# Identity matmuls of TensorE ahead of nine of its waits, in a kernel of three layers

## The chip, the core and the metric

The kernel runs on one core of a Trainium2 chip. The metric is the device time of one execution in microseconds; lower is better. The engines are named as in the profile: PE is TensorE's matmuls and PEld its weight loads, DVE is VectorE, ACT is ScalarE, POOL is GpSimd, SP issues DMAs.

## The reference

256 tokens of width 2048 pass through an attention layer, a retention layer and a second block (attention of two kinds, then a feed-forward with a convolution), everything in float32. Cut to what matters:

```python
def first_block(x, ...):
    x = layer_norm(ALPHA * x + attention_mixer(x, ...), gain[0], bias[0])   # 16 heads of 128, 4 kv heads
    x = layer_norm(ALPHA * x + retention_mixer(x, ...), gain[1], bias[1])   # 8 heads, 256 and 512 wide
    return x

def second_block(x, c, ...):
    mod = silu(c) @ w_mod + b_mod                      # six rows of 2048
    h = rms_norm(x, norm_attn) * (1 + sc1) + sh1
    x = x + g1 * (concat(swa_attention(...), dsa_attention(...)) @ w_out)
    h = rms_norm(x, norm_ffn) * (1 + sc2) + sh2
    u, g = split(h @ w_up)                             # 2 x 5632 columns
    x = x + g2 * ((silu(causal_conv3(u) + conv_b) * g) @ w_down)
    return rms_norm(x, norm_final)
```

Every projection `h @ w` is computed by the kernel as a sum of three products of rounded parts, `x_hi w_hi + x_hi w_lo + x_lo w_hi`.

## The kernel before, in words

Weights are cut into blocks of 2048x512 (some narrower), and a block into four chunks of 512 rows. For every chunk SP issues two DMAs into `raw`, ScalarE rounds it to `w_hi` (`round_hi`, line 389), VectorE subtracts to get `w_lo` (`split_lo`, line 394, written over `raw`), and TensorE multiplies (`product`, lines 400 to 402; `project` for the x-side projections, `output` for those behind a head). A chunk of `project` is 4 slices x 2 token tiles x 3 products = 24 matmuls of 128x512. `raw`, `w_hi` and `w_lo` hold four chunks; SP waits for TensorE's semaphore `products` before it loads one anew. Each engine has its own queue, written out by hand, and works it in order; semaphores tie them together.

TensorE's queue is that of `pe_first_block` and `pe_second_block`. Attention has a first step written out (`pe_attention(pe, 0)`) and a loop over the other three key-value heads; then come the last head's transposes (`pe_a_turn`) and output (`pe_a_output`). `turn_groups` brings the activations into the layout for products: eight groups of four 128x128 results, in six banks in turn (`turn[0]`, `turn[1]`, `sc[0]`, `sc[1]`, `pair[1][0]`, `pair[1][1]`), as plain transposes (line 466) or as f32 matmuls with the diagonal matrix `diag` (line 464), which scales as it transposes. VectorE turns each group to `x_mid` (line 496), ScalarE rounds it to `x_hi` (line 477), VectorE makes `x_lo` (line 483), and the first chunk of the next product waits for two groups' `x_lo`. Retention has the same form as attention, with eight steps. In its first step VectorE also scales the residual rows (`vec_residual`) before it splits the next block's fourth chunk. The second block follows: `diag` of the first RMS norm, projections, index and attention heads, output, `diag` of the second, and the feed-forward in 11 steps (`pe_feed_forward`), whose last output is `pe_f_output(pe, FG)`; it waits for `f_hl`, which comes from `f_h` by way of `f_hh`, and `f_h` from the convolution (`f_conv`).

The matrix `ident` is 128x128 f32 in SBUF. The banks are PSUM banks of 128x512 f32; eight exist: two `pair`s of two, two `turn`, two `sc`.

The calls of TensorE's queue that the change stands among, with the lines of before:

```python
            if first:                                   # in pe_attention
                for c in range(CH):
                    between(c)
            else:
                pe_a_output(pe, i, between)
...
                            mm = pe.matmul(to, src, diag[:, t, :], start=True, stop=True)   # L464
                        else:
                            mm = pe.transpose(to, src, ident[:, :])                         # L466
```

Of the kernel before, what the change touches and what calls it, by code (L numbers as in the profile page):

```python
# [25 lines left out]
P = 128  # L26
# [13 lines left out]
FG = FF // CB  # L40
# [75 lines left out]
def build(nc, x, attn_w_in, attn_q_gain, attn_k_gain, attn_w_out, ret_w_in, ret_decay_exp,  # L116
# [5 lines left out]
    with ctx:  # L122
# [24 lines left out]
        ident = take("ident", [P])  # L147
# [126 lines left out]
        def bank(name):  # L274
            return ctx.enter_context(nc.psum_tensor(name, [P, CB], F32))

        pair = [[bank("pair0_t0"), bank("pair0_t1")], [bank("pair1_t0"), bank("pair1_t1")]]
        turn = [bank("turn0"), bank("turn1")]
        sc = [bank("sc0"), bank("sc1")]
# [3 lines left out]
        def sem(name):  # L283
            if name not in S:
                S[name] = ctx.enter_context(nc.semaphore(name))
            return S[name]
# [216 lines left out]
        def pe_transposes(pe, to, src, tiles):  # L503
# [4 lines left out]
                    mm = pe.transpose(to[:, i * P:(i + 1) * P], src[:, t, m * P:(m + 1) * P], ident[:, :])  # L508
            return mm

        def pe_mod(pe, step):

            pe.wait_ge(sem("mod_used"), 8 * step + 8)
            for q in range(8):
                mm = pe.matmul(sc[0][:, q:q + 1], m_acc[:, q * P:(q + 1) * P],  # L515
                               ones[:, 0:1], start=True, stop=True)
            mm.then_inc(sem("mod_cols"), 1)
# [5 lines left out]
        def pe_a_output(pe, i, after=None):  # L523

            last = isinstance(i, int) and i == A_KV

            def before(c):
                if c == 0:
                    pe.wait_ge(sem("a_ol"), 2 * i)
                    pe.wait_ge(sem("a_sg"), i if last else i + 1)  # L530
                elif c == 1:
                    if not last:
                        pe.wait_ge(sem("a_krot"), i + 1)
                else:
                    pe.wait_ge(sem("a_sum_z"), 2 + 4 * (i - 1) + c - 1)
            output(pe, a_block(i, 0) if last else a_block(i, 3), a_oh, a_ol, [0, 1, 0, 1], before, after)

        def pe_a_turn(pe, i):

            pe.wait_ge(sem("a_og"), i)  # L540
            for b in range(2):
                pe_transposes(pe, turn[b], a_og, [2 * b, 2 * b + 1]).then_inc(sem("a_turned"), 1)

        def pe_attention(pe, i):
# [84 lines left out]
            def between(c):  # L629

                if c == 1:
                    turn_probs(0)
                    turn_probs(1)
                elif c == 2:
                    pe.wait_ge(sem("a_prob"), 4 * i + 4)
                    values(0)
                    turn_probs(2)
                    values(1)
                    turn_probs(3)
                elif c == 3:  # L640
                    values(2)
                    values(3)
            project(pe, a_block(i, 2), pair[0], before=q_read, after=along_gate)
            if first:
                for c in range(CH):
                    between(c)
            else:
                pe_a_output(pe, i, between)

# [19 lines left out]
        def pe_r_output(pe, i, after=None):  # L669
            last = isinstance(i, int) and i == R_HEADS  # L670

            def before(c):
                if c == 0:
                    pe.wait_ge(sem("r_ol"), 2 * i)
                    pe.wait_ge(sem("r_sg"), i if last else i + 1)
                elif c == 1:
                    if not last:
                        pe.wait_ge(sem("r_v"), i + 1)
                else:
                    pe.wait_ge(sem("r_sum_z"), 2 + 4 * (i - 1) + c - 1)  # L680
            output(pe, r_block(i, 0) if last else r_block(i, 3), r_oh, r_ol, [0, 1, 0, 1], before, after)

        def pe_r_turn(pe, i):
            pe.wait_ge(sem("r_og"), i)
            for b in range(2):
                pe_transposes(pe, turn[b], r_og, [2 * b, 2 * b + 1]).then_inc(sem("r_turned"), 1)

        def pe_retention(pe, i):
            first = isinstance(i, int) and i == 0

            def arrived(c):
                if first:
                    pe.wait_ge(sem("turn_lo"), 8 + 2 * (c + 1))
                elif c == 0:
                    pe.wait_ge(sem("r_sg"), i)
                    pe.wait_ge(sem("r_sum_z"), 2 + 4 * (i - 1) - 1)

            def mod(c):
                if c == 1:
                    pe_mod(pe, A_KV + i - 1)  # L700
            project(pe, r_block(i, 0), pair[0], before=arrived)
            if not first:
                pe_r_turn(pe, i)

            def v_free(c):
                if c == 0 and not first:
                    pe.wait_ge(sem("r_v"), i)
                    pe.wait_ge(sem("r_sum_z"), 2 + 4 * (i - 1))
            project(pe, r_block(i, 1), pair[1], before=v_free, after=mod)

            def qk_read(c):
                if c == 0:
                    pe.wait_ge(sem("r_rot"), i + 1)

            def along_gate(c):

                if c == 0:
                    if not first:
                        pe.wait_ge(sem("r_ol"), 2 * i)
                    pe_transposes(pe, turn[0], r_qk, [0, 1]).then_inc(sem("r_qk_turned"), 1)  # L720
                    pe_transposes(pe, turn[1], r_qk, [2, 3]).then_inc(sem("r_qk_turned"), 1)
                elif c == 2:
                    pe.wait_ge(sem("r_qT"), i + 1)
                    pe.wait_ge(sem("r_kT"), i + 1)
                    if not first:
                        pe.wait_ge(sem("r_og"), i)
                    pe.wait_ge(sem("mod_read"), A_KV + i)
                    for s in range(NT):
                        for k in range(2):
                            mm = pe.matmul(sc[0][:, s * T:(s + 1) * T], r_kT[:, k, s * P:(s + 1) * P],  # L730
                                           r_qT[:, k, :], start=k == 0, stop=k == 1)
                    mm.then_inc(sem("r_score"), 1)
                elif c == 3:
                    pe.wait_ge(sem("r_s"), i + 1)
                    pe.wait_ge(sem("r_v"), i + 1)
                    for t in range(NT):
                        for s in range(NT):
                            mm = pe.matmul(sc[t][:, :], r_s[:, s, t * P:(t + 1) * P], r_v[:, s, :],  # L738
                                           start=s == 0, stop=s == NT - 1)
                    mm.then_inc(sem("r_o"), 1)  # L740
            project(pe, r_block(i, 2), pair[0], before=qk_read, after=along_gate)
            if not first:
                pe_r_output(pe, i)

        def pe_first_block(pe):
            pe.wait_ge(sem("ident_in"), 16)
            pe_turn_x(pe, 0)
            pe_turn_x(pe, 1)
            pe_attention(pe, 0)
            with pe.Fori(1, A_KV) as i:  # L750
                pe_attention(pe, i)
            pe_a_turn(pe, A_KV)
            pe_a_output(pe, A_KV)
            def normalized(j):
                if j % 4 == 0:
                    pe.wait_ge(sem("z_norm"), j // 4 + 1)
                    pe.wait_ge(sem("z_norm1"), j // 4 + 1)
            turn_groups(pe, 1, normalized, False)
            pe_retention(pe, 0)
            with pe.Fori(1, R_HEADS) as i:  # L760
                pe_retention(pe, i)
            pe_r_turn(pe, R_HEADS)
            pe_r_output(pe, R_HEADS)


        def act_attention(act, i, n, rest):
# [924 lines left out]
        def pe_f_output(pe, f, after=None):  # L1691
            last = isinstance(f, int) and f == FG

            def before(c):
                if c == 0:
                    pe.wait_ge(sem("f_hl"), f)
                    pe.wait_ge(sem("f_u"), f if last else f + 1)
                if c == 1:
                    pe.wait_ge(sem("f_g"), f if last else f + 1)
                if c >= 2:  # L1700
                    pe.wait_ge(sem("f_scaled"), 2 + 4 * (f - 1) + c - 1)
            output(pe, f_block(f, 0) if last else f_block(f, 2), f_hh, f_hl, [0, 1, 0, 1], before, after)
# [36 lines left out]

        def pe_second_block(pe):  # L1740
            pe_second_attention(pe)
            pe.wait_ge(sem("diag"), 2)
            turn_groups(pe, 3, lambda j: None, True)
            pe_feed_forward(pe, 0)
            with pe.Fori(1, FG) as f:
                pe_feed_forward(pe, f)
            pe_f_output(pe, FG)


# [679 lines left out]
```

## Time and profile before

| | |
|---|---|
| median of 3 runs | 2398.57 us (2394.43 to 2398.9) |
| profiled execution | 2398.79 us |
| its span, first to last instruction | 2396.8 us |
| mean granted TensorE clock | 0.977 |
| PE busy | 2286.5 us (95%), 10702 matmuls |
| PEld busy | 1882.0 us (79%) |
| DVE busy | 1668.0 us (70%) |
| ACT busy | 986.7 us (41%) |
| POOL busy | 134.7 us (6%) |
| the costliest lines | L400 to L402 with x_hi and x_lo: 2112 matmuls each, 825.1, 810.6 and 811.0 us |

Durations of matmuls overlap, since they are pipelined: the distance from start to start, not the duration, is what one takes from the engine. A row of the timeline gives the start, the duration of the whole merged group, what ran, and in brackets how long the engine had been idle before it and what ended that. The granted clock (PEclk) is 1.00 for 2.4 GHz and 0.50 for 1.2 GHz.

### The profile page before, as it was taken

How to read it: one execution, taken by the hardware profiler on the slowest of the kernel's cores; microseconds unless marked ns; L12 is line 12 of the kernel's file. 1: busy time of each engine (PE TensorE's matmuls, PEld its weight loads, DVE VectorE, ACT ScalarE, POOL GpSimd, SP SyncE). 2: the span in 40 equal slices, each digit the busy share in tenths (PEclk: the TensorE clock that was granted, in tenths of full speed). 3: DMA queues.
4: the chain of work that ended last, by engine and by line, in shares of the span. 5: the costliest groups of instructions: out<-in, count | busy, mean ns of one | idle time of the engine just before them, and what ended most of it. 6: DMA issues, size and time to landing. Idle time of an engine off the chain costs nothing.

```text
span 2396.8 us, 28967 instructions
## 1 busy us (share of the span) xinstructions
PE 2286.5 (95%) x10702; PEld 1882.0 (79%) x10702; DVE 1668.0 (70%) x1841; ACT 986.7 (41%) x1001; POOL 134.7 (6%) x193
## 2 busy tenths in 40 slices
PE   7799998989999999999879999998999999999996
PEld 6688886878878888788668777877888888888885
DVE  6688877886867877768773556795566666666666
ACT  4543442333344334433333445444444444444442
POOL 2100010000000000000001000000000000000000
PEclk9999998999999999999988999999999999999998
DMA  7777776687778777778636444454555555555552
GB/s 256 270 246 255 252 254 210 212 283 249 276 243 277 248 261 281 244 251 274 229 98 203 145 132 132 135 194 140 174 192 191 182 188 192 183 184 192 182 189 102
DMA packets 262119, 503.38 MB, mean 210 GB/s; under 512 B 16801, under 2 KB 70353, under 8 KB 261168
## 3 DMA queue, kind: packets, MB, share of 16 engines
q1 hardware_dynamic: 230656, 382.39, 48.6%
q0 software_dynamic: 31120, 119.14, 14.3%
q10 hardware_dynamic: 288, 1.11, 0.1%
q8 instruction: 35, 0.57, 0.1%
q14 instruction: 20, 0.16, 0.0%
HBM read 498.90 MB, written 3.69 MB: 210 GB/s over the span
## 4 chain that ended last, share of the span: by engine, by line
PE 55%; issue 35%; DVE 4%; DMA 3%; ACT 2%; POOL 0%; SPq 0%; ACTq 0%; DVEq 0%; POOLq 0%
PE pair_t L400 16%; PE pair_t L402 15%; PE pair_t L401 15%; DMA raw<-in_attn_w_in_dram 1%; PE turn L508 1%; PE sc L1502 1%; PE sc L738 1%; ACT w_hi L389 1%; DVE w_lo L394 1%; DVE m_acc L981 1%; PE sc L515 1%; PE sc L730 1%; DMA m_raw<-in_w_mod_dram 1%; PE turn L1510 0%; PE sc L594 0%
## 5 line engine op out<-in xcount | busy, mean ns | idle before, releaser
L394 DVE TENSOR_TENSOR w_lo<-raw,w_hi 128x2048 fp32r<-128x2048 f32 (+1 forms) x371 | 824.6, 2225 | 563.4 <-ACT w_hi L389 558.4
L389 ACT ACTIVATE w_hi<-raw 128x2048 fp32r<-128x2048 f32 (+1 forms) x371 | 690.8, 1864 | 1114.9 <-DMA raw<-in_ret_w_in_dram 372.2
L400 PE MATMUL pair_t<-w_hi,x_hi 128*128 128x512 f32 (+2 forms) x2112 | 825.1, 391 | 20.4 <-DVE w_lo L394 19.3
L402 PE MATMUL pair_t<-w_hi,x_lo 128*128 128x512 f32 (+2 forms) x2112 | 811.0, 384 | 0.0
L401 PE MATMUL pair_t<-w_lo,x_hi 128*128 128x512 f32 (+2 forms) x2112 | 810.6, 384 | 0.0
L400 PEld LDWEIGHTS pair_t<-w_hi,x_hi 128*128 128x128 f32 x2112 | 401.8, 190 | 106.7 <-DVE w_lo L394 21.0
L402 PEld LDWEIGHTS pair_t<-w_hi,x_lo 128*128 128x128 f32 x2112 | 401.5, 190 | 78.3
L401 PEld LDWEIGHTS pair_t<-w_lo,x_hi 128*128 128x128 f32 x2112 | 402.1, 190 | 73.8 <-issue 0.2
L981 DVE SCALAR_TENSOR_TENSOR m_acc<-m_raw,csilu,m_acc 128x1024 f32<-128x1024 f32 x180 | 230.8, 1282 | 5.2 <-DMA m_raw<-in_w_mod_dram 1.8
L400 PE MATMUL pair_t<-w_hi,f_hh 128*128 128x512 f32 x352 | 140.2, 398 | 7.0 <-DVE f_hl L2228 7.0
L402 PE MATMUL pair_t<-w_hi,f_hl 128*128 128x512 f32 x352 | 138.3, 393 | 0.0
L401 PE MATMUL pair_t<-w_lo,f_hh 128*128 128x512 f32 x352 | 138.0, 392 | 0.0
L1404 POOL DMA_DIRECT2D m_raw<-in_w_mod_dram x96 | 69.0, 719 | 960.3 <-DVE m_acc L981 945.6
L400 PE MATMUL pair_t<-w_hi,r_oh 128*128 128x512 f32 x256 | 104.6, 408 | 7.9 <-DVE r_ol L1151 7.9
L401 PE MATMUL pair_t<-w_lo,r_oh 128*128 128x512 f32 x256 | 101.5, 396 | 0.0
L402 PE MATMUL pair_t<-w_hi,r_ol 128*128 128x512 f32 x256 | 101.5, 396 | 0.0
L400 PEld LDWEIGHTS pair_t<-w_hi,f_hh 128*128 128x128 f32 x352 | 66.7, 189 | 21.0 <-DVE f_hl L2228 7.4
L402 PEld LDWEIGHTS pair_t<-w_hi,f_hl 128*128 128x128 f32 x352 | 66.5, 189 | 15.4
L401 PEld LDWEIGHTS pair_t<-w_lo,f_hh 128*128 128x128 f32 x352 | 66.6, 189 | 13.9
L1138 DVE TENSOR_TENSOR z<-z,pair_t 128x512 f32<-128x512 f32 x96 | 61.4, 681 | 19.7 <-PE pair_t L402 19.7
L400 PEld LDWEIGHTS pair_t<-w_hi,r_oh 128*128 128x128 f32 x256 | 48.6, 190 | 20.9 <-DVE r_ol L1151 8.2
L1995 DVE TENSOR_TENSOR f_y<-pair_t,rows 128x512 f32<-128x512 f32 x88 | 56.4, 683 | 9.6 <-PE pair_t L402 9.6
(333 smaller groups left out, 2051.9 us busy)
## 6 DMA issues: line engine op xcount, KB each, us to landing
m_raw<-in_w_mod_dram POOLq DMA_DIRECT2D x96, 1024.0 KB, 7.1
raw<-in_ret_w_in_dram SPq DMA_DIRECT2D x192, 512.0 KB, 4.6
raw<-in_w_up_dram SPq DMA_DIRECT2D x176, 512.0 KB, 4.2
raw<-in_w_down_dram SPq DMA_DIRECT2D x88, 512.0 KB, 4.5
raw<-in_attn_w_in_dram SPq DMA_DIRECT2D x64, 512.0 KB, 4.9
raw<-in_ret_w_out_dram SPq DMA_DIRECT2D x64, 512.0 KB, 4.7
raw<-in_w_in_dram SPq DMA_DIRECT2D x56, 512.0 KB, 4.7
raw<-in_attn_w_out_dram SPq DMA_DIRECT2D x32, 512.0 KB, 5.1
```

Source lines behind the costliest of these rows:

```text
L389: act.activation(chunk(w_hi, c, width), chunk(raw, c, width), ACT.Copy).then_inc(sem("hi"), 1)
L394: v.tensor_tensor(chunk(w_lo, c, width), chunk(raw, c, width), chunk(w_hi, c, width).bitcast(F32), ALU.subtract).then_inc(sem("lo"), 1)
L400: pe.matmul(to, xh, wh, start=start, stop=False)
L401: pe.matmul(to, xh, wl, start=False, stop=False)
L402: return pe.matmul(to, xl, wh, start=False, stop=stop)
L508: mm = pe.transpose(to[:, i * P:(i + 1) * P], src[:, t, m * P:(m + 1) * P], ident[:, :])
L515: mm = pe.matmul(sc[0][:, q:q + 1], m_acc[:, q * P:(q + 1) * P], ones[:, 0:1], start=True, stop=True)
L730: mm = pe.matmul(sc[0][:, s * T:(s + 1) * T], r_kT[:, k, s * P:(s + 1) * P], r_qT[:, k, :], start=k == 0, stop=k == 1)
L981: ins = v.scalar_tensor_tensor(out=m_acc[:, :], in0=w, scalar=cc, in1=m_acc[:, :], op0=ALU.mult, op1=ALU.add)
L1138: ins = v.tensor_tensor(z[:, t, c * CB:(c + 1) * CB], z[:, t, c * CB:(c + 1) * CB], pair[order[c]][t][:, :], ALU.add)
L1404: g.dma_start(m_raw[:, u % 2, :, :], w_m[:, 2 * u:2 * u + 2, bass.ds(2 * step * CB, 2 * CB)])\
L1995: ins = v.tensor_tensor(tmp[:, t, :], banks[t][:, :], rows[:, row, c * CB:(c + 1) * CB], ALU.mult)
```

## The change

A helper `pe_fill(pe, to, n)` issues n matmuls of `ident` by `ident` into the first 128 columns of a bank; nobody reads the result. It is called nine times: in attention's first step, 38 between two parts of the heads' work (after `between(1)`) and 45 at its end; 29 before the last `pe_a_turn` and 47 after `pe_a_output(pe, A_KV)`; 54 after `pe_retention(pe, 0)`; 60 between the last `pe_r_turn` and `pe_r_output`, and 146 after that; 72 before the wait for the second `diag`; and 54 before the last `pe_f_output`, with a wait for the last `f_conv` ahead of them. That is 545 calls. Nothing else differs.

```diff
--- before.py
+++ after.py
@@ -508,6 +508,11 @@
                     mm = pe.transpose(to[:, i * P:(i + 1) * P], src[:, t, m * P:(m + 1) * P], ident[:, :])
             return mm
 
+        def pe_fill(pe, to, n):
+
+            for _ in range(n):
+                pe.matmul(to[:, 0:P], ident[:, :], ident[:, :], start=True, stop=True)
+
         def pe_mod(pe, step):
 
             pe.wait_ge(sem("mod_used"), 8 * step + 8)
@@ -644,6 +649,9 @@
             if first:
                 for c in range(CH):
                     between(c)
+                    if c == 1:
+                        pe_fill(pe, pair[1][0], 38)
+                pe_fill(pe, pair[1][0], 45)
             else:
                 pe_a_output(pe, i, between)
 
@@ -749,18 +757,23 @@
             pe_attention(pe, 0)
             with pe.Fori(1, A_KV) as i:
                 pe_attention(pe, i)
+            pe_fill(pe, turn[0], 29)
             pe_a_turn(pe, A_KV)
             pe_a_output(pe, A_KV)
+            pe_fill(pe, turn[0], 47)
             def normalized(j):
                 if j % 4 == 0:
                     pe.wait_ge(sem("z_norm"), j // 4 + 1)
                     pe.wait_ge(sem("z_norm1"), j // 4 + 1)
             turn_groups(pe, 1, normalized, False)
             pe_retention(pe, 0)
+            pe_fill(pe, pair[1][0], 54)
             with pe.Fori(1, R_HEADS) as i:
                 pe_retention(pe, i)
             pe_r_turn(pe, R_HEADS)
+            pe_fill(pe, sc[0], 60)
             pe_r_output(pe, R_HEADS)
+            pe_fill(pe, turn[0], 146)
 
 
         def act_attention(act, i, n, rest):
@@ -1739,11 +1752,14 @@
 
         def pe_second_block(pe):
             pe_second_attention(pe)
+            pe_fill(pe, turn[0], 72)
             pe.wait_ge(sem("diag"), 2)
             turn_groups(pe, 3, lambda j: None, True)
             pe_feed_forward(pe, 0)
             with pe.Fori(1, FG) as f:
                 pe_feed_forward(pe, f)
+            pe.wait_ge(sem("f_conv"), FG)
+            pe_fill(pe, turn[0], 54)
             pe_f_output(pe, FG)
```

## Rows read from the trace of the kernel before

**Rows 1.** The page, part 1: busy us, share of the span, matmuls.
```profile
PE 2286.5 (95%) x10702; PEld 1882.0 (79%) x10702; DVE 1668.0 (70%) x1841; ACT 986.7 (41%) x1001; POOL 134.7 (6%) x193
```
**Rows 2.** Timeline of TensorE at the first `diag`: start us, duration us, work [idle before].
```profile
1234.46 3.78 PE L464 MATMUL turn<-diag,z 128*128 128x128 f32 x16 [17.57 <-DVE diag L1979]
...
1240.88 1.95 PE L464 MATMUL pair_t<-diag,z 128*128 128x128 f32 x16
1242.67 1.95 PE L464 MATMUL turn<-diag,z 128*128 128x128 f32 x16
```
**Rows 3.** Groups by line and shape: count | busy us, mean ns | idle before, releasers.
```profile
L464 PE MATMUL turn<-diag,z 128*128 128x128 f32 x64 | 11.5, 353 | 26.5 <-DVE diag L1979 26.5
...
L466 PE MATMUL turn<-ident,z 128*128 128x128 f32 x32 | 6.0, 349 | 12.1 <-ACT z L896 6.4 <-DMA z<-in_x_dram 5.7
```
**Rows 4.** Timeline of TensorE at block (1,0), fourth chunk.
```profile
120.98 0.80 PE L400 MATMUL pair_t<-w_hi,x_hi 128*128 128x512 f32 x1 [6.07 <-DVE w_lo L394]
121.58 0.63 PE L401 MATMUL pair_t<-w_lo,x_hi 128*128 128x512 f32 x1
...
122.86 0.63 PE L401 MATMUL pair_t<-w_lo,x_hi 128*128 128x512 f32 x1
...
124.13 0.39 PE L401 MATMUL pair_t<-w_lo,x_hi 128*128 128x512 f32 x1
...
124.81 0.40 PE L401 MATMUL pair_t<-w_lo,x_hi 128*128 128x512 f32 x1
```
**Rows 5.** Timelines at the other waits, and of ScalarE ahead of 120.98.
```profile
91.16 1.20 PE L612 MATMUL sc<-a_v,a_pT 128*128 128x128 f32 x4 [5.37 <-ACT a_pT L819]
...
111.67 3.71 ACT L916 ACTIVATE rows<-rows 128x2048 f32<-128x2048 f32 x2 [7.23 <-DMA rows<-in_ln_bias_dram]
...
384.37 1.97 PE L508 MATMUL turn<-ident,a_og 128*128 128x128 f32 x8 [4.20 <-DVE a_og L1128]
387.75 0.79 PE L400 MATMUL pair_t<-w_hi,a_oh 128*128 128x512 f32 x1 [1.41 <-DVE a_ol L1145]
...
522.57 0.80 PE L400 MATMUL pair_t<-w_hi,x_hi 128*128 128x512 f32 x1 [6.99 <-DVE w_lo L394]
...
1192.86 0.79 PE L400 MATMUL pair_t<-w_hi,r_oh 128*128 128x512 f32 x1 [7.95 <-DVE r_ol L1151]
...
2359.33 0.80 PE L400 MATMUL pair_t<-w_hi,f_hh 128*128 128x512 f32 x1 [6.99 <-DVE f_hl L2228]
```
**Rows 6.** Stretches: length, PE, PEld, DVE, ACT, POOL busy, PEclk, DMA share, GB/s.
```profile
89.97:96.79 6.82, 5.63 (x26) 5.66 (x27) 5.33 (x6) 3.03 (x8) 1.46 (x2) 0.50 0.42 134
117.27:124.10 6.83, 3.12 (x7) 2.49 (x8) 5.43 (x4) 4.17 (x4) 0.00 (x0) 0.50 0.17 46
383.51:393.75 10.24, 7.97 (x22) 6.32 (x23) 4.48 (x7) 3.10 (x3) 2.89 (x4) 0.50 0.55 193
419.57:424.47 4.90, 4.90 (x23) 4.90 (x24) 3.86 (x9) 2.96 (x4) 0.00 (x0) 0.50 0.00 0
520.04:526.87 6.83, 4.30 (x10) 3.43 (x11) 6.80 (x5) 1.91 (x1) 1.09 (x2) 0.50 0.82 316
1189.06:1195.88 6.82, 3.02 (x7) 2.44 (x8) 5.94 (x5) 2.88 (x3) 0.53 (x1) 0.50 0.46 154
1219.78:1240.26 20.48, 5.80 (x27) 5.80 (x28) 13.29 (x17) 5.26 (x6) 4.02 (x3) 0.50 0.11 39
1615.72:1625.96 10.24, 4.12 (x19) 4.13 (x20) 4.34 (x9) 4.88 (x15) 0.71 (x1) 0.50 0.41 162
2356.41:2363.24 6.83, 3.91 (x9) 3.15 (x10) 5.15 (x3) 1.91 (x1) 0.00 (x0) 0.50 0.09 34
...
1298.28:1311.94 13.66, 13.66 (x58) 12.96 (x58) 6.91 (x4) 7.17 (x6) 0.00 (x0) 0.50 0.90 295
```
**Rows 7.** Timeline of VectorE at the normalized turns.
```profile
420.72 1.90 DVE L496 TENSOR_SCALAR x_mid<-turn,par 128x256 f32<-128x256 f32 x4 [1.04 <-PE turn L466]
...
424.95 0.68 DVE L483 TENSOR_TENSOR x_lo<-x_mid,x_hi 128x512 fp32r<-128x512 f32 x1
```

## The prediction, made before the changed kernel was run

> **What bounds the kernel now.** I read the page's busy shares first: TensorE (PE) is busy for 2286.5 of 2396.8 us [rows 1], so it sets the time nearly everywhere. What it can give back lies in two places: the 110.3 us in which it has nothing to do, and stretches in which it works at the lower clock. So the second view is its timeline around long waits. Nine waits of 4 us and more stand in it, as the rows give them: 5.37, 6.07, 4.20, 6.4, 6.99, 7.95, 17.57, 8.93 (26.5 less 17.57) and 6.99 us [rows 2 to 5], 70.5 us in all. The change has nine calls of `pe_fill`, one for each. The third view is the granted clock by windows: during each of these waits it falls from 1.00 to 0.50 (2.4 to 1.2 GHz), and it stays there for some microseconds of work after the wait [rows 6]. The reader should see in [rows 2] what that costs: the same `diag` matmuls that come 32 in 6.42 us at first (1234.46 to 1240.88) come 16 in 1.79 us afterwards.
>
> A wait is counted in idle time after the last matmul's modelled end. New matmuls start earlier, one spacing after the last start: a 128x512 lasts 0.39 and comes every 0.227 us (124.13 to 124.81, three spacings) [rows 4]. So each wait has room for its idle time plus 0.16 us; nine waits hold 71.9 us.
>
> **The price of one fill.** The trace of before has no ident-by-ident matmul. The nearest row is line 464, the same call with the same shape, 128x128 f32 by 128x128 f32, no transpose. The source makes 64 such calls (2 rounds of `turn_groups`, 32 each), 32 of them into the two `turn` banks (groups 0, 1, 6, 7), and the trace has 64 instructions there: each call is two instructions. The transposes of line 466, again two rounds and 32 calls into `turn`, have 32: one each [rows 3]. `pe_fill` calls `pe.matmul`, not `pe.transpose`. An instruction costs 1.79/16 = 0.112 us at the full clock [rows 2], so one fill costs 0.224 us, and 545 fills 122.0 us. Its bounds are one instruction, 0.112 us, and two at the lower clock, 32 in 6.42 us or slower, so above 0.40 us. I take 0.224, since all of the form, the types and the size are those of line 464.
>
> The Trainium skill (TensorE: Matmul & The Clock Gate, Part 1, "Wait — 56ns, not 53.3ns?") gives 55.6 ns from start to start for back-to-back matmuls of 128 columns. By that figure 545 fills would be an estimated 30 us, less than half of the waits. The trace's row for this form has 0.112 us for each of two instructions, so it disagrees for f32, and the measurement decides.
>
> **Site by site.** Fill, less room, less the clock regained. For work left behind the wait at 0.50 I take 47% of its busy time where it is 128x512 (0.427 us at the low clock, 121.58 to 122.86, against 0.227) [rows 4] and half where it is 128x128 f32 [rows 2].
> 1. 38 fills in attention's first step: 8.50 - 5.53 = +2.97. The cold stretch holds 5.63 us of work, -2.8. Net +0.2.
> 2. 45 fills: they stand before block (1,0), three chunks of 24 matmuls (16.3 us) ahead of the wait at its fourth chunk. That wait ends at 120.98 because ScalarE rounds the weights only after it has scaled `rows`, which waits for a DMA [rows 5]; TensorE has no part in it, so fill and wait can overlap although they are apart. 10.07 - 6.23 = +3.84; 3.12 us cold, -1.5. Net +2.3.
> 3. 29 before `pe_a_turn`: 6.49 - 4.36 = +2.13. Cold 7.97 us, of which about 2 are transposes followed by a 1.41 us wait for `a_ol` [rows 5], which stays. I take 6.0 x 0.47 + 0.5 = -3.3. Net -1.2.
> 4. 47 before the normalized turns: 10.52 - 6.56 = +3.96. Here 4.90 us are cold transposes, but VectorE is the pace: from its first `x_mid` (420.72) it works without a gap to the second `x_lo` (424.95 + 0.68), which the first product needs [rows 7]. Only the first group's turn gets shorter, -0.45. Net +3.5.
> 5. 54 after `pe_retention(0)`, again three chunks ahead of its wait: 12.08 - 7.15 = +4.93; 4.30 cold, -2.0. Net +2.9.
> 6. 60 after `pe_r_turn`: 13.43 - 8.11 = +5.32; 3.02 cold, -1.4. Net +3.9.
> 7. 146 before the first `diag`: 32.67 - 17.73 = +14.94; 32 instructions in 3.6 instead of 6.4 us, -2.8. Net +12.1.
> 8. 72 before the second: 16.11 - 9.09 = +7.02; 4.12 cold, -2.1. Net +4.9.
> 9. 54 before the last `f_hl`, behind a new wait for `f_conv`. Behind it are queued the fills and then the products that wait for `f_hl`; since VectorE writes `f_conv` before `f_h`, and `f_hl` is made from `f_h`, the new wait ends long before the old one. I cost it at nothing; had it still to be waited for, the fills would start that much later. 12.08 - 7.15 = +4.93; 3.91 cold, -1.8. Net +3.1.
>
> The sum is 50.0 of overrun less 18.2 of clock regained, +31.8 us. The clock gain lies between nothing, if the engine isn't kept at 2.4 GHz, and some 21 (all busy time of [rows 6] but the last row, halved or at 47%, without the limits of sites 3 and 4). Nothing is moved or removed: no DMA, no other engine's instruction. Other engines are idle longer behind a late TensorE, which costs nothing by itself. The overrun is not hidden: after each site products on TensorE follow, 95% busy over the kernel.
>
> Does the fill keep the clock? In the first `diag` turns nothing but line 464 ran from 1234.46 on, and the clock came back at 1240.26 in the midst of it [rows 2, 6]; so this form counts. The Trainium skill says in the same page (Part 4: PE-mode transpose) that transposes don't bring 2.4 GHz. The trace disagrees: at 424.47 it came back with only transposes of line 466 behind it since 419.57 [rows 6]. By the rule the turns after sites 3 and 4 might lose it again, an estimated 3 us more.
>
> **Rivals.**
> A. The fills end ahead of their waits (the other side). If one fill is one instruction, 545 x 0.112 = 61.0 us fit into 71.9, with every fill shorter than its room. Then only the clock is regained, without site 1, whose gain the wait of site 2 swallows: 18.2 - 2.8 = 15.4, so 2383.4. It decides at the price of one fill: (71.9 + 18.2)/545 = 0.165 us is where it neither gains nor loses. For it: every count times 0.112 comes out a little under its wait. Against it: 64 instructions for 32 calls [rows 3].
> B. The clock isn't held by a fill of zeros and ones, or by this form. PE busy is no proof of the clock: it fell to 0.50 at 1298.28 with the engine busy all through, 58 matmuls in 13.66 us [rows 6], those of the 80-column block at first. At site 7 it fell 2.9 us after the last work (1234.46 - 17.57 to 1219.78) [rows 2, 6]; if each fill ran 3 us at full and the rest at half speed, they would take 2 x 122 - 9 x 3 = 217 us, less 71.9, +145, so 2544. Against it: 1240.26 above.
> C. The fill is much cheaper still, by the page's 55.6 ns: the trace's waits of 4.20 us already lose the clock, and what is left of each wait behind such fills is near that. By rows: as with no change, 2395 to 2399.
> D. Overrun that is given back later. All other idle time of TensorE is 110.3 - 70.5 = 39.8 us, its start and the kernel's tail among it; waits on work that doesn't depend on TensorE, as at site 2, would shrink. If a quarter goes, -10: 2420.6.
>
> **How the numbers follow.** Forecast as summed 0.78, A 0.06, B 0.04, C 0.04, D 0.08. The profiled execution took 2398.79 us for a span of 2396.8, the median of the runs is 2398.57, so 0.2 us lower; 2398.8 + 31.8 = 2430.6. The range reaches from D less another 4 us (2416) to 9 us above the forecast (2440), which takes in a clock regained only by half; A, B and C stay out. 0.2% is 4.8 us, about what a measurement of this kernel can tell from no change: faster 0.06 (A), same 0.04 (C), slower 0.90 (B, D and the forecast).
>
> **What would show it.** The fill's line should have 1090 matmuls, spaced 0.112 us; half as many mean A. Each of the nine waits should be gone, with the fill's end 2 to 15 us later than the wait ended. The granted clock should stay 1.00 at all nine, and still fall in the 80-column products. At sites 2 and 5 the fill should stand 16 us ahead of where the wait was. At site 4 the second `x_lo` should be ready about 5.6 us after the first transpose, against 425.63 - 419.57 = 6.1. TensorE's busy time should grow by about 122 less 18 us. If the clock falls within a fill, B holds; if the span grows by much less than the overruns, D does. What would make me wrong most is the price of one fill.

## The result, and the profile after

| | before | after |
|---|---|---|
| median | 2398.74 us (2394.43 to 2399.44, 4 runs) | 2434.21 us (2432.8 to 2436.69, 4 runs) |
| profiled execution, its span | 2398.79, 2396.8 us | 2432.8, 2430.9 us |
| mean granted clock | 0.977 | 0.993 |
| PE busy | 2286.5 us | 2389.2 us |

The ratio is 1.0157, 95% interval 1.0143 to 1.0171: by the medians the changed kernel is slower by 35.5 us, where 31.8 were forecast; the two profiled executions differ by 34.0. The mean clock rose and TensorE is busy for 102.7 us more, and both are bought with instructions that nobody needs.

The page, part 1, of the kernel after, answers to [rows 1]. Other engines' busy times are those of before to within 0.2 us, and TensorE has 1090 instructions more (11792 less 10702):
```profile
PE 2389.2 (98%) x11792; PEld 1989.1 (82%) x11792; DVE 1668.1 (69%) x1841; ACT 986.5 (41%) x1001; POOL 134.7 (6%) x193
```
The groups of the fill's line, L514 (count | busy us, mean ns | idle before), show what one fill costs. 348 calls into `turn` are 696 instructions, 137 into `pair[1][0]` are 274, 60 into `sc[0]` are 120. 123.2 us for 545 calls make 0.226 each, as worked out from line 464 in [rows 2] and [rows 3] (a group's busy time holds the end of its last matmul too, hence the last 1%):
```profile
L514 PE MATMUL turn<-ident 128*128 128x128 f32 x696 | 78.5, 275 | 0.0
L514 PE MATMUL pair_t<-ident 128*128 128x128 f32 x274 | 31.1, 275 | 0.0
L514 PE MATMUL sc<-ident 128*128 128x128 f32 x120 | 13.6, 275 | 0.0
```
TensorE's timeline at site 7 answers to [rows 2] (start, duration, work). In place of 17.57 us of idle time stand 292 matmuls of `ident`, 32.77 us long; then 16 `diag` matmuls come in 1.79 us at once (1259.30 to 1261.09), with none of the slow ones:
```profile
1226.70 32.77 PE L514 MATMUL turn<-ident 128*128 128x128 f32 x292
1259.30 1.95 PE L464 MATMUL turn<-diag,z 128*128 128x128 f32 x16
1261.09 1.17 PE L464 MATMUL sc<-diag,z 128*128 128x128 f32 x9
```
The windows (length, busy times with counts, PEclk, DMA share, GB/s) answer to [rows 6]. The first is the fill of site 7, with the clock at 1.00 all through; the two others are new low stretches which the forecast didn't have, behind the waits that follow sites 4 and 8 (the second at the first `f_g`):
```profile
1226.60:1259.30 32.70, 32.70 (x295) 32.65 (x293) 13.97 (x17) 5.69 (x5) 4.01 (x3) 1.00 0.13 40
...
428.12:431.54 3.42, 3.42 (x10) 2.65 (x9) 3.42 (x8) 1.26 (x2) 0.00 (x0) 0.50 0.02 5
1708.12:1711.54 3.42, 3.42 (x12) 2.85 (x10) 1.94 (x3) 3.41 (x3) 0.00 (x0) 0.50 0.00 1
```
All nine waits are gone from the list of TensorE's waits (who waited for whom: us in total, times, longest). What leads it now, apart from the first load, is short or was there before:
```profile
PE turn L466 <- DMA z<-in_x_dram: 5.9, 1, 5.9
PE sc L508 <- ACT f_g L1951: 4.1, 1, 4.1
PE pair_t L400 <- DVE w_lo L394: 2.8, 3, 1.6
...
PE pair_t L400 <- DVE x_lo L483: 1.9, 1, 1.9
```
The same matmul, fills left out, can be found in both timelines. How much later it starts after the change, ahead of each site and behind it once the clock is back, gives each site's cost:

```
site           start before -> after           shift    start before -> after           shift   cost   forecast
1 and 2          85.51 ->   83.11   ahead      -2.41     125.96 ->  126.12   behind     +0.16   +2.6   +2.5
3               379.90 ->  379.77              -0.13     394.30 ->  392.82              -1.48   -1.3   -1.2
4               412.81 ->  411.33              -1.48     429.90 ->  433.46              +3.56   +5.0   +3.5
5               498.19 ->  501.78              +3.58     527.88 ->  534.24              +6.36   +2.8   +2.9
6              1184.64 -> 1190.88              +6.24    1197.82 -> 1207.87             +10.05   +3.8   +3.9
7              1216.49 -> 1226.46              +9.97    1242.00 -> 1263.99             +21.99  +12.0  +12.1
8              1612.48 -> 1635.35             +22.87    1626.91 -> 1654.68             +27.78   +4.9   +4.9
first f_g      1675.26 -> 1703.01             +27.76    1683.00 -> 1713.69             +30.69   +2.9    0
9              2351.94 -> 2382.94             +31.00    2364.92 -> 2398.90             +33.99   +3.0   +3.1
```

The lead of 2.41 us ahead of site 1 is none of the change's: the weights of the fourth chunk of block (0,1), an early wait on DMAs and VectorE, came earlier in that execution (1.55 us of waiting against 4.61). In the other kernels' executions, where nothing was put into it, that wait was 1.55 to 4.07 us long, and it may be one source of the spread between runs of one kernel (2389.94 to 2403.07 us for the kernel before). The lead reached site 2 as well: ScalarE began to scale `rows` at 108.57, where it was 111.67 before, so the +2.6 of sites 1 and 2 is counted against a kernel before that would have been as much ahead. Before the first fill the clock was at 0.50 once, from 66.31 for 3.41 us; in the kernel before it had been so from 49.01 for 6.83 us.

Between sites 7 and 8 the shift grows by 0.9 us more. The wait ahead of `i_kdup`, behind the 80-column block, took 2.34 us instead of 1.34 (at 1340.08); the forecast has no term for it.

### The profile page after: what moved, and what is told of

Its sections match the earlier page's. It is cut to its first block, busy times and chain, and to the rows that moved or that the text cites. A ratio compares the mean times of both kernels' runs of the same rounds, so it can differ in the third digit from the quotient of the medians.

```text
span 2430.9 us, 31147 instructions
## 1 busy us (share of the span) xinstructions
PE 2389.2 (98%) x11792; PEld 1989.1 (82%) x11792; DVE 1668.1 (69%) x1841; ACT 986.5 (41%) x1001; POOL 134.7 (6%) x193
## 4 chain that ended last, share of the span: by engine, by line
PE 63%; issue 32%; DVE 2%; DMA 1%; ACT 1%; POOL 0%; SPq 0%; ACTq 0%; POOLq 0%; DVEq 0%
PE pair_t L400 17%; PE pair_t L402 17%; PE pair_t L401 17%; PE turn L514 2%; PE pair_t L514 1%; PE turn L508 1%; PE sc L746 1%; PE sc L1515 1%; PE sc L520 1%; PE sc L617 1%; ACT w_hi L389 1%; PE sc L599 1%; PE sc L738 1%; PE sc L514 1%; DMA raw<-in_attn_w_in_dram 1%
## 5 line engine op out<-in xcount | busy, mean ns | idle before, releaser
L514 PEld LDWEIGHTS turn<-ident 128*128 128x128 f32 x696 | 78.4, 192 | 0.3
L514 PE MATMUL turn<-ident 128*128 128x128 f32 x696 | 78.5, 275 | 0.0
L402 PEld LDWEIGHTS pair_t<-w_hi,f_hl 128*128 128x128 f32 x352 | 66.1, 188 | 13.7
```

Source lines behind the costliest of these rows:

```text
L402: return pe.matmul(to, xl, wh, start=False, stop=stop)
L514: pe.matmul(to[:, 0:P], ident[:, :], ident[:, :], start=True, stop=True)
```

## The experiments

Each differs from the changed kernel as its diff says. Each ratio is to runs of the kernel before that were taken along with that kernel's; their median was 2399.12 us for the first four kernels and 2397.54 for the others. The theory was that the price of a fill, two instructions or 0.224 us, decides alone, and that a fill that ends ahead of its wait gives the clock back for nothing.

**Half the counts at all nine sites.**
```diff
-                        pe_fill(pe, pair[1][0], 38)
+                        pe_fill(pe, pair[1][0], 19)
-                pe_fill(pe, pair[1][0], 45)
+                pe_fill(pe, pair[1][0], 22)
...
-            pe_fill(pe, turn[0], 146)
+            pe_fill(pe, turn[0], 73)
```


> All nine sites keep their fills, at half the counts (19, 22, 14, 23, 27, 30, 73, 36, 27: 271 calls). My theory: the change was slower only by the price of a fill, 0.224 us for two instructions. 271 fills take 60.7 us and each set ends about 1.2 us ahead of its wait, so nothing is added and the clock is regained: about 15 us less than before, less up to 3 for later waits that grow: 2383 to 2388. Rival: filling costs by itself, because it keeps TensorE's queue busy at bad moments (late products, later DMAs) and the clock gives little back: half of the change's cost stays, about 2410 to 2417. Second rival: the clock falls anyway, since an idle rest of 1.2 us follows each set: 2396 to 2401.

Measured: 2385.61 us (2384.07 to 2388.8), ratio to before 0.9951, interval 0.9936 to 0.9967. Half the work of the change turns a loss of 35.5 us into a gain of 12 to 14. Both rivals fall: filling costs nothing by itself, and the clock holds at every site but one. At site 2 the rest behind the fill was 2.16 us, and the clock was 0.50 from 120.17 for 3.41 us. TensorE's timeline at site 7 shows a fill that ends ahead of the wait, 1.30 us of idle time, and then `diag` matmuls at the full clock:
```profile
1208.63 16.46 PE L514 MATMUL turn<-ident 128*128 128x128 f32 x146
1226.39 2.05 PE L464 MATMUL turn<-diag,z 128*128 128x128 f32 x16 [1.30 <-DVE diag L1995]
```
The window around it has the granted clock at 1.00:
```profile
1208.00:1227.00 19.00, 17.70 (x155) 17.38 (x154) 14.66 (x18) 5.92 (x5) 4.01 (x3) 1.00 0.21 67
```

**Transposes at the full counts.**
```diff
-                pe.matmul(to[:, 0:P], ident[:, :], ident[:, :], start=True, stop=True)
+                pe.transpose(to[:, 0:P], ident[:, :], ident[:, :])
```


> All nine sites at the full counts (545), but each fill is a transpose of ident by ident, one instruction of 0.11 us instead of two. My theory: 545 instructions take about 60 us, as in the halved kernel, and the clock came back behind transposes alone at 424.47 in the kernel before, so they hold it: 2383 to 2388, within 2 us of the halved kernel. Rival, by the Trainium skill (TensorE: Matmul & The Clock Gate, Part 4: PE-mode transpose), transposes do not count as activity for the clock: it falls at all nine waits as before, 2396 to 2402.

Measured: 2384.45 us (2381.05 to 2388.53), ratio 0.9944, interval 0.9926 to 0.9961. The count of calls is the change's and the time is that of half the counts, so it is the number of instructions that costs: a transpose is one. The group of the fill in this kernel, at the `turn` banks:
```profile
L514 PE MATMUL turn<-ident 128*128 128x128 f32 x348 | 38.8, 273 | 0.0
```
Its window at site 7:
```profile
1208.00:1227.00 19.00, 17.46 (x153) 16.90 (x152) 15.12 (x19) 5.93 (x5) 4.01 (x3) 1.00 0.21 69
```
348 instructions for 348 calls, 0.111 us each, and a granted clock of 1.00 with hardly anything but transposes running. As with half the counts, the clock fell at site 2 alone (120.76), behind a rest of 2.51 us. The Trainium skill's rule that transposes don't bring the full clock (TensorE: Matmul & The Clock Gate, Part 4: PE-mode transpose) would have given the 2396 to 2402 of the rival; the trace disagrees.

**Only site 7, at 146 and at 73.**
```diff
-            pe_fill(pe, turn[0], 29)
+            pe_fill(pe, turn[0], 0)
...
             pe_fill(pe, turn[0], 146)
...
-            pe.wait_ge(sem("f_conv"), FG)
```


> Only the 146 fills before the first diag are kept. My theory: 32.6 us of fills in a wait with room for 17.7, less 2.8 us for turns at the full clock: +12.1, so 2409 to 2412. Rival: part of the change's cost comes from sites together (the order of late work), and one alone costs less than 8 us.

Measured: 2412.83 us (2409.36 to 2413.84), ratio 1.0058, interval 1.0038 to 1.0078: 13.7 us slower, for 12.1 expected; the median lies 0.8 us above the range that was given. One site alone makes more than a third of the whole loss.

> Only site 7, with 73 fills, 16.3 us in a wait with room for 17.7. My theory: no overrun, turns at the full clock: -2.8, so 2395 to 2397; 14.9 us less than with 146. Rival: the diag chain of the other engines is slowed by TensorE writing banks beside it, so that the wait itself grows and the time is 2399 or more.

Measured: 2396.84 us (2391.17 to 2402.82, 10 runs), ratio 0.9993, interval 0.998 to 1.0006. The median lies where it was expected, but a gain of 2.8 us can't be told from none by it. Matched as in the table of shifts, the same products ahead of site 7 and behind it tell it apart from the spread of the rest: +12.0 us with 146 fills, -2.8 us with 73. The medians differ by 16.0 us for 14.9 expected. The wait's end isn't pushed out, since the first `diag` matmul starts 17.7 us after the fill does (1209.84 to 1227.53), and in [rows 2] the wait held as much. TensorE writing a bank beside the other engines' work did not slow the chain to `diag` here.
```profile
1209.84 16.46 PE L514 MATMUL turn<-ident 128*128 128x128 f32 x146
1227.53 2.05 PE L464 MATMUL turn<-diag,z 128*128 128x128 f32 x16 [1.23 <-DVE diag L1994]
```

**A quarter of the counts at all nine sites** (9, 11, 7, 11, 13, 15, 36, 18, 13).

> All nine sites at a quarter of the counts (9, 11, 7, 11, 13, 15, 36, 18, 13: 133 calls, 29.8 us in 71.9 us of room), so that 2.6 to 9.6 us of each wait stay idle behind the fills. This is what the fills would be at the price of rival C. My theory: the idle rests alone decide: those over about 4 us (sites 2, 4 to 9) still lose the clock, so at most sites 1 and 3 gain, some 3 us: 2393 to 2399. Rival: fills early in a wait carry the clock through the rest, and the time is that of the halved counts, 2384 to 2388.

Measured: 2396.67 us (2392.75 to 2399.16, 10 runs), ratio 0.9999, interval 0.9988 to 1.001: no gain. The rests behind the fills were 2.63 to 9.49 us, and the clock fell at all nine places, at sites 1 and 3 too, where I had allowed for a gain. So a fill at the start of a wait didn't carry the clock through the rest. At site 7, 9.49 us stay idle behind 36 fills, and the first 16 `diag` matmuls take 3.26 us (1234.40 to 1237.66) instead of 1.79:
```profile
1216.71 8.20 PE L514 MATMUL turn<-ident 128*128 128x128 f32 x72
1234.40 3.43 PE L464 MATMUL turn<-diag,z 128*128 128x128 f32 x16 [9.49 <-DVE diag L1995]
1237.66 1.95 PE L464 MATMUL sc<-diag,z 128*128 128x128 f32 x16
```
The window has the clock at 0.50 again:
```profile
1227.10:1237.30 10.20, 2.90 (x13) 2.90 (x14) 5.10 (x8) 3.07 (x4) 0.71 (x1) 0.50 0.01 2
```

**Half the counts, and the 80-column block multiplied 256 columns wide.**
```diff
-            project(pe, B_B0 + 2, pair[0], width=80)
+            project(pe, B_B0 + 2, pair[0], width=256)
```


> The halved counts, and the block of 80 columns (B_B0 + 2) multiplied 256 columns wide by TensorE, the columns from 80 on being leftovers that nobody reads. In the kernel before its 80-column products came every 0.111 us at the full clock and every 0.213 at the low one, and the clock fell to 0.50 in the midst of them with the engine busy. Theory: what holds the clock is the columns that stream, not that the engine is busy; 96 or so wider products at about 0.12 us cost 1 us more, the clock stays at 1.00 through the block, and half of 13.7 us comes back: 2379 to 2381. Rival: the clock fell there for another reason (a wait of 1.3 us close by, contention with DMAs at a share of 0.97): 2385 to 2388, with the clock at 0.50 as before.

Measured: 2383.75 us (2381.82 to 2385.81), ratio 0.9945, interval 0.9926 to 0.9964. The theory is right on the clock and wrong on the time. The clock stays at 1.00 through the block, where it was 0.50 for 13.66 us in [rows 6] and for as long with half the counts. The rival of contention with DMAs is out: their share over the widened block (1277.40 to 1289.00) is 0.98, as high as it was before. The window around it:
```profile
1270.00:1291.00 21.00, 20.05 (x138) 18.50 (x136) 4.83 (x7) 5.23 (x7) 1.66 (x3) 1.00 0.79 254
```
But the next thing that TensorE needs, `i_kdup`, is copied by VectorE only after four chunks of `w_lo`, which come one in 2.9 us (1291.78, 1294.77, 1297.63) at the pace at which `raw` lands. So the time gained is waited away: 3.58 us idle at this point in TensorE's timeline.
```profile
1300.54 0.44 PE L508 MATMUL sc<-ident,i_kdup 128*128 128x128 f32 x2 [3.58 <-DVE b_w L2062]
```
The same place in the kernel with half the counts alone, 1.21 us idle:
```profile
1306.05 0.44 PE L508 MATMUL sc<-ident,i_kdup 128*128 128x128 f32 x2 [1.21 <-DVE b_w L2062]
```
After the longer wait the clock fell to 0.50 at 1301.03 for 3.41 us, which took back more. Against the kernel before, the same matmuls start 14.6 us earlier ahead of the block (1272.97), 18.9 us earlier at the last product ahead of `i_kdup` (1296.56) and 14.6 us again at 1344.15, so the widening gained nothing in the end. That the median is 1.9 us under that of half the counts can't be told from none.

**Counts fitted to the waits, and three more sets.** The counts are 24, 28, 19, 29, 32, 36, 79, 40, 32; the added calls:
```diff
+                if c == 3 and first:
+                    pe_fill(pe, turn[0], 8)
...
+            pe_fill(pe, pair[0][0], 8)
             pe_retention(pe, 0)
...
+                    if first:
+                        pe_fill(pe, pair[0][0], 12)
                     pe.wait_ge(sem("f_g"), f + 1)
```


> Counts fitted to the rooms at 0.224 us each (24, 28, 19, 29, 32, 36, 79, 40, 32), and three more sets at waits of some 2 to 4 us at which the clock still fell in the halved kernel: 8 before the fourth chunk of block (0,1), 8 behind the normalized turns, 12 before the first f_g. Theory: the fit adds nothing, closes the rest at site 2, and the three low-clock stretches of 3.4 us or more go, 1.6 us each: 4 to 6 us less than with halved counts, 2379 to 2382. Rival: these short falls come back elsewhere because VectorE or a DMA sets the pace there: no gain over the halved counts, 2384 to 2388.

Measured: 2383.08 us (2379.5 to 2384.78), ratio 0.9939, interval 0.9917 to 0.9961. The clock doesn't fall any more at the three added places, nor at site 2; a window behind the normalized turns has it at 1.00, where it was 0.50 at 428.12 in the changed kernel:
```profile
414.00:425.00 11.00, 10.84 (x48) 8.94 (x48) 11.00 (x17) 4.57 (x6) 0.00 (x0) 1.00 0.30 95
```
The median is 2.5 us under that of half the counts and the intervals overlap, so the 4 to 6 us expected did not come. The matched matmuls of the profiled execution show where they went. Site 4 gave 0.6 us instead of costing 0.9, and the first `f_g` cost nothing instead of 1.5. But the 80-column block was slow for longer, 17.07 us from 1279.10: the lead over the kernel before shrank there from 17.2 to 14.0 us, where with half the counts it stayed at 11.0 to 11.1. Why the low stretch was longer stays open.

**Both together.**

> The fitted counts with the three more sets, and the 256-column block together. If both gains are real and independent they add: 2373 to 2376. If one of them is only moved into a later wait, the time is that of the better of the two, 2379 to 2382.

Measured: 2384.16 us (2380.65 to 2385.56), ratio 0.9939, interval 0.9919 to 0.9959. The gains don't add. The mean granted clock is 0.997, the highest of all kernels here, and the time no better than at 0.991: TensorE waits 3.6 us for `i_kdup`, as in the widened kernel. It also waits 3.75 us for a chunk of `w_lo` at 141.78, where the fitted kernel waited 1.39; that stands far ahead of the block and isn't the widening's (the waits of this kernel, as above):
```profile
PE pair_t L400 <- DVE w_lo L394: 8.3, 5, 3.8
...
PE sc L508 <- DVE b_w L2067: 3.6, 1, 3.6
```

The kernels by the instructions of `pe_fill` (in the fitted one 56 of them stand at the three added places):

| kernel | instructions of fill | mean clock | median us | ratio to before |
|---|---|---|---|---|
| before | 0 | 0.977 | 2398.74 | 1 |
| a quarter | 266 | 0.982 | 2396.67 | 0.9999 |
| half | 542 | 0.991 | 2385.61 | 0.9951 |
| transposes, full counts | 545 | 0.991 | 2384.45 | 0.9944 |
| fitted, three more sets | 694 | 0.994 | 2383.08 | 0.9939 |
| the change | 1090 | 0.993 | 2434.21 | 1.0157 |

## Why the prediction was right

**The price of a fill.** It carried everything, and it was right: 1090 instructions, 0.112 us from start to start (32.60 us from the first fill of site 7 to the first `diag`, over 292). Rival A put the other side at 0.165 us a call; the transposes, at 0.111, landed on that side at 2384.45, where A's own sum was 2383.4. The 55.6 ns of the Trainium skill (TensorE: Matmul & The Clock Gate, Part 1), measured there with bf16, don't carry over to f32: the trace has twice that per instruction, and two instructions.

**The sites.** Seven of the eight sums, taking 1 and 2 together, hit within 0.2 us, as the table of shifts shows. That includes both fills that stand three chunks ahead of their wait: the wait at 120.98 ended without TensorE's part, so a fill 16 us away filled it. The whole came out near the forecast partly by luck: the costs of the table add up to 35.7 us, the wait ahead of `i_kdup` puts in another 1.0, and the early lead of 2.4 us, which no term foresaw, hid part of it in the profiled execution.

**Site 4** cost 5.0 us instead of 3.5. The step that failed is its clock term. I counted 0.45 us regained and nothing lost. The turns did go at the full clock, and the second `x_lo` came 5.55 us after the first transpose, for 5.6 forecast. Up to the first product behind them the sum held: it started 1.97 us later than before (427.66 against 425.69), which from -1.48 is +3.45. But TensorE was done early and waited 1.95 us for `x_lo`, as VectorE was the pace (it was named as such, but only to limit the gain); and the clock fell at 428.12 behind this wait, which slowed the first ten products and cost the other 1.6 us:
```profile
424.67 1.04 PE L466 MATMUL turn<-ident,z 128*128 128x128 f32 x8
427.66 0.50 PE L400 MATMUL pair_t<-w_hi,x_hi 128*128 128x512 f32 x1 [1.95 <-DVE x_lo L483]
428.73 0.63 PE L400 MATMUL pair_t<-w_hi,x_hi 128*128 128x512 f32 x1
```
In the kernel before, slow turns had hidden that wait: 0.03 us of idle time stood ahead of the product at 425.69. The fill moved the fall of the clock, it did not remove it. That the same fall stood in the kernels with half the counts (420.55) and with transposes (421.13), and went when 8 fills were put into the wait, shows this.

**The first f_g** cost 2.9 us that the sum did not have. TensorE waited 4.07 us instead of 2.77, since ScalarE's rounding ahead of `f_g` had to wait for a chunk of `raw` (first line), and then the clock fell for 3.42 us, as shown above:
```profile
1704.54 1.91 ACT L389 ACTIVATE w_hi<-raw 128x2048 fp32r<-128x2048 f32 x1 [4.83 <-DMA raw<-in_w_up_dram]
...
1707.47 1.40 PE L508 MATMUL sc<-ident,f_g 128*128 128x128 f32 x8 [4.07 <-ACT f_g L1951]
```
Whether the landing was late because of the change stays open. In the other kernels without fills there this wait was 2.65 to 3.07 us, and the clock fell at it in five of them (half, transposes, both of site 7, widened) and neither in the quarter's nor before, with 2.65 and 2.77 us. So 1.3 of the 2.9 us, the longer wait, may be of this execution alone. The rest is the fall of the clock, which cost 1.5 us with half the counts too, at a wait no longer than before.

**The clock regained.** The sum had 18.2 us, or 15.4 where every fill ends ahead of its wait. Half the counts gained 0.49% (0.33 to 0.64%), 11.8 us with an interval of 8 to 15, which by itself can't be told from 15.4. Its profiled execution, matched with that of the kernel before, tells where the two part (shift behind less shift ahead, as in the table above; the forecast is the regained clock alone):

```
site               1 and 2     3      4      5      6      7      8    first f_g    9
half the counts     -1.5     -3.4   +0.9   -2.0   -1.6   -2.7   -2.0     +1.5     -1.9
forecast            -1.5     -3.3   -0.45  -2.0   -1.4   -2.8   -2.1      0       -1.8
```

Seven of the eight terms came within 0.2 us. The 2.8 us missing are the falls that came anew at site 4 and at f_g.

**Rivals B, C and D.** B, the clock not held, is out: 1.00 in every fill. C, fills that are too short, is what the quarter shows, and its time of 2395 to 2399 came: 2396.67. D, overrun given back later, gave back hardly anything: TensorE's wait at 143.95 shrank from 1.61 us to 0.70, since its end didn't move (143.98), but another of 0.53 came in at 140.14. The sum was 3.6 us short of the median (3.8, had it started from the median of 2398.57 and not from the profiled execution), and what it lacked lies at site 4 and f_g. At site 4 that is a wait laid bare by a faster TensorE, the opposite of D.

## What to carry to other kernels

Work that keeps an engine warm has a price per call that must be read off the trace for its exact form, and the number of instructions per call is part of it; here it was two for an f32 matmul and one for a transpose, and this factor alone turned a gain of 0.5% into a loss of 1.6%. A fill should end a little ahead of its wait's end: what it lasts too long costs one for one on the bounding engine, and one that leaves too long a rest gives nothing (behind the fills here, rests of up to 1.7 us kept the clock and rests of 2.2 us and more lost it). And when a slow stretch is made fast, look at once for the wait that it was hiding, since the clock, or the time, may be lost there again: the widened block gained 4 us and gave them back within 50 us.

## What was not expected of the hardware

- A wait of 1.95 us, behind 3.7 us of transposes, was followed by a fall of the clock (428.12), and so was one of 2.16 us with half the counts (at 120.17), while one of 2.77 us was not in the kernel before (1678.42). A wait of 2.65 us at this last place was followed by a fall with half the counts and by none with a quarter, so the length of the wait alone doesn't decide. By the waits of the kernel before alone, 4.20 us and more, I had taken short ones for harmless.
- TensorE, busy without a gap on the 80-column block, was granted 0.50 for 13.66 us; on the same block multiplied 256 columns wide it was granted 1.00, in both kernels that have it. The first was to be seen in the kernel before; the second took the widened kernel.
- A higher mean clock need not be a shorter time: 0.991 and 2385.61 us, 0.997 and 2384.16 us, 0.993 and 2434.21 us.
